# Attention's set-up over eight PSUM banks, small weights scaled earlier, and expert outputs added into the residual in DRAM

## The reference

```python
mod = silu(c) @ w_ada + b_ada                       # six vectors of 1024
h = modulate(rms_norm(x, norm1_g), sh1, sc1)
q_c, kv_c, k_r, u, b_gate, c_gate = split(h @ w_in) # 256, 128, 32, 512, 512, 512
attn = mla_mixer(...)      # 8 heads; keys 64 + 32 rotary; mask by chunks of 64
conv = b_gate * (short_conv(c_gate * u) + conv_b)
x = x + g1 * (concat(rms_norm(attn), rms_norm(conv)) @ w_out)
h2 = modulate(rms_norm(x, norm2_g), sh2, sc2)
x = x + g2 * hier_moe(h2)  # 4 groups x 8 experts, best 2 of the best group
return rms_norm(x, final_g)
```

## Time and profile before

| | us |
|---|---|
| median of 3 runs (2191.21 to 2192.27) | 2191.83 |
| profiled execution, its own time | 2191.35 |
| its span in the trace | 2189.6 |
| TensorE busy (matmul) | 1880.3, 86% |
| VectorE busy | 1234.1, 56% |
| ScalarE busy | 702.4, 32% |
| GpSimd busy | 641.9, 29% |
| data moved by DMA | 307.54 MB, 140 GB/s |

### The profile page before, as it was taken

One profiled execution on the slowest core, in us unless ns is written; L12 is line 12 of the kernel. 1 busy time (PEld: TensorE's weight loads), 2 busy tenths in 40 slices (PEclk: granted clock), 3 DMA queues, 4 the chain that ended last, 5 costly groups with the idle time before them and its releaser, 6 DMA issues. The chain is left out here.

```text
span 2189.6 us, 26611 instructions
## 1 busy us (share of the span) xinstructions
PE 1880.3 (86%) x8674; PEld 1448.1 (66%) x8674; DVE 1234.1 (56%) x1938; ACT 702.4 (32%) x1091; POOL 641.9 (29%) x662
## 2 busy tenths in 40 slices
PE   2999999937999999999997699992999999999900
PEld 2677878814656656656655488882998899998800
DVE  5667576555775775776775644435333343333359
ACT  2435343202333333333333233220223322223234
POOL 5677776601211211211211311100232333323100
PEclk9999999966999999999999699996999999999955
DMA  7555656300000000000000444424788887888478
GB/s 288 178 158 169 183 143 173 106 33 1 8 8 5 7 7 5 7 7 5 7 7 27 157 160 147 150 96 145 247 270 273 277 278 270 278 265 274 164 300 332
DMA packets 214685, 307.54 MB, mean 140 GB/s; under 512 B 22901, under 2 KB 166480, under 8 KB 212314
## 3 DMA queue, kind: packets, MB, share of 16 engines
q1 hardware_dynamic: 191002, 228.99, 32.3%
q0 software_dynamic: 18944, 69.21, 8.7%
q10 hardware_dynamic: 4672, 8.56, 1.0%
HBM read 245.91 MB, written 60.82 MB: 140 GB/s over the span
## 5 line engine op out<-in xcount | busy, mean ns | idle before, releaser
L823 PE MATMUL tbank<-KR,VV 128*128 128x512 f32 (+3 forms) x640 | 299.3, 549 | 27.2 <-DVE on L919 27.2
L1015 ACT ACTIVATE KR<-tbank 128x512 f32<-128x512 f32 (+1 forms) x320 | 170.3, 532 | 334.1 <-PE tbank L800 330.9
L903 DVE TENSOR_REDUCE cmax<-tbank 128x1 f32<-128x512 f32 (+2 forms) x340 | 205.8, 607 | 76.9 <-PE tbank L761 67.5
L1038 POOL TENSOR_SCALAR diag<-cst,nmax 128x128 fp32r<-128x128 f32 x138 | 84.1, 610 | 533.4 <-DVE nmax L906 533.4
L798 PE MATMUL tbank<-Qhi,Khi 97*128 97x512 f32 (+2 forms) x321 | 216.9, 676 | 0.0
L348 PE MATMUL pbank<-hhi,wslhi 128*128 128x512 f32 x512 | 205.5, 401 | 4.5 <-DVE wsllo L399 2.8
L1724 DVE TENSOR_SCALAR xTe<-ebank,modcol 128x256 f32<-128x256 f32 (+1 forms) x128 | 53.7, 472 | 260.4 <-PE ebank L1644 139.2
L348 PE MATMUL pbank<-hhi,wsllo 128*128 128x512 f32 x512 | 200.0, 391 | 0.0
L348 PE MATMUL pbank<-hlo,wslhi 128*128 128x512 f32 x512 | 199.6, 390 | 0.0
L1666 PE MATMUL ebank<-xTe,wg 128*128 128x192 f32 x1024 | 171.8, 326 | 3.1 <-DVE ahi L1752 1.8
L1666 PEld LDWEIGHTS ebank<-xTe,wg 128*128 128x128 f32 x1024 | 167.9, 190 | 7.8 <-DVE aT L1748 2.1
(11 more groups left out here) (261 smaller groups left out, 3517.7 us busy)
## 6 DMA issues: line engine op xcount, KB each, us to landing
wg<-in_w_exp_gate SPq DMA_DIRECT2D x32, 1024.0 KB, 5.9
wu<-in_w_exp_up SPq DMA_DIRECT2D x32, 1024.0 KB, 10.2
wd<-in_w_exp_down SPq DMA_DIRECT2D x32, 1024.0 KB, 7.7
wraw<-in_w_in SPq DMA_DIRECT2D x60, 512.0 KB, 3.8
wmod<-in_w_ada POOLq DMA_DIRECT2D x16, 1024.0 KB, 7.0
y<-y_dram SPq DMA_DIRECT2D x16, 1024.0 KB, 21.3
wada<-in_w_ada SPq DMA_DIRECT2D x2, 4096.0 KB, 22.5
xt<-in_x SPq DMA_DIRECT2D x4, 2048.0 KB, 12.4
```

What stands on the lines that cost most here:

```text
L823: ins = pe.matmul(out, VV[:, kt, 2 * b:2 * b + 2].rearrange("p c d -> p (c d)"), step_of(probs, m), start=kt == 0, stop=last)
L903: W(ve.tensor_reduce(cmax[:, i % 2, n:n + 1], plain[:, chunk % 2, 0:w], AX.X, ALU.max), plain_read)
L1015: A(act.activation(step_of(probs, m), scores[:, m % 2, j * P:512], ACT.Exp), exp_done)
```

## The change

It makes three groups of edits.

In **project**, the loads of w_uq, w_uk and w_uv come after the three broadcast rows, ahead of the loop that loads slices, and their scaling goes to VectorE at group 2, slice 14. For room, buffers are shared (`xsq` with `hf`, `uc` with `sq[:, 0]`, `t4` with `conv[:, 1]`), with three more waits, and `LATE` is 32: 32 steps of 128 columns.

In **attend**, the first head's keys go to banks 0 to 3 and its queries to banks 4 to 7, without waits between them; values follow in freed banks. Constant rows move from VectorE to ScalarE (mask rows, rotary high part) and GpSimd (zero rows, fills of VV), those of the second buffer later. `probs` has a buffer of its own.

In **route, experts and combine**, gates are split in three bfloat16 parts and carried as marks (6 x 32 columns), so that each slot has its gate. VectorE now takes both outputs out of PSUM and multiplies them by gate and g2row. GpSimd adds the rows to x2_dram with an accumulating indirect DMA; each scatter waits until the previous expert's has landed, and the b rows go for each expert apart. y_dram is gone, and combine only loads x2, normalises and stores, on SP, with four result buffers.

```diff
-LATE = 16
+LATE = 32
...
+            q = T["w_uq"].rearrange("l (k p) n -> p (l k) n", p=P)
+            sp.dma_start(wuq[:, :, 0:HEADS * QKD], q).then_inc(ld_up, 16)
...
+                    if (n, s) == (2, 14):
+                        ve.wait_ge(ld_up, 16 * 6)
+                        for k in range(KQ):
+                            V(ve.tensor_scalar(wuq[:, k], wuq[:, k], cols[:, R_Q + k:R_Q + k + 1], SM, ALU.mult, ALU.mult))
+                        V(ve.tensor_scalar(wuk[:], wuk[:], cols[:, R_KV:R_KV + 1], None, ALU.mult))
+                        V(ve.tensor_scalar(wuv[:], wuv[:], cols[:, R_KV:R_KV + 1], None, ALU.mult))
...
+            for n in range(4):
+                pe.matmul(bank[0:NOPE, n], wk[:, 0], kvn[:, n * 512:(n + 1) * 512], start=True, stop=True
+                          ).then_inc(made_done, 1)
+            for n in range(4):
+                for k in range(KQ):
+                    ins = pe.matmul(bank[:, 4 + n], wq[:, 0, k], qn[:, k, n * 512:(n + 1) * 512],
+                                    start=k == 0, stop=k == KQ - 1)
+                ins.then_inc(made_done, 1)
+            for v in range(V_EARLY):
+                pe.wait_ge(made_dve, V_EARLY_AFTER[v])
+                make_values(v, 0, bank[:, V_EARLY_BANK[v]])
...
+            rope_low(0)
             W.wait()
             for chunk in range(AHEAD):
                 maximum(chunk, chunk)
+            rope_low(1)
...
+            for n in range(4):
+                part(2 * n + 1, 0, 0)
+                if n < V_EARLY:
+                    copy_values(n, 0, bank[:, V_EARLY_BANK[n]])
+                mask_rows(0, n)
+            rope(1)
             for g in range(GROUPS_AHEAD):
                 copy_maxima(g, 0, 0)
+            for n in range(4):
+                mask_rows(1, n)
...
+            zero = cst[QKD:QKD + 1, C_ID:C_ID + 1].to_broadcast([1, S])
+            for b in range(2):
+                for k, lows in enumerate((Klo, Qlo)):
+                    po.tensor_scalar(lows[QKD:QKD + 1, b], zero, 0.0, None, ALU.mult).then_inc(rows_pool, 1)
+                    po.wait_ge(rows_pool, 2 * b + k + 1)
+                if b == 0:
+                    for k in (1, 3):
+                        po.memset(VV[:, :, k], 1.0).then_inc(filled, 1)
+                        po.wait_ge(filled, k // 2 + 1)
+                    for n in range(4):
+                        rest(n, 0, 0)
+                    po.wait_ge(qlo_done, 4)
...
+            for i, left in enumerate((gates, gleft[:, 0], gleft[:, 1])):
+                do(ve.tensor_copy(gpart[:, i], left if i else gates[:]))
+                if i < 2:
+                    do(ve.tensor_tensor(gleft[:, i], left if i else gates[:], gpart[:, i], ALU.subtract))
+                for k in range(2):
+                    do(ve.tensor_tensor(marks[:, :, k, (3 + i) * NEXP:(4 + i) * NEXP], pick[:, :, k],
+                                        across(gpart[:, i, k::2].unsqueeze(2), NT, NEXP), ALU.mult))
...
-                po.indirect_dma_start(out=y_dram, in_=y, in_offset=None,
+                po.indirect_dma_start(out=x2_dram, in_=y, in_offset=None, compute_op=ALU.add,
...
+                hold(po, st_ya[1 - b], r * (PAIRS * 16) + q * 16 + b * 16, passed_pool)
+                hold(po, st_yb[1 - b], r * (PAIRS * 16) + q * 16 + b * 16, passed_pool)
                 hold(po, ya_done, r * NEXP + q * 2 + (b + 2), passed_pool)
                 put(ya[:, b], ja[:, b:b + 1], st_ya[b])
+                hold(po, yb_done, r * NEXP + q * 2 + (b + 2), passed_pool)
+                put(yb[:, b], jb[:, b:b + 1], st_yb[b])
...
+                ve.scalar_tensor_tensor(ya[:, b], outa.rearrange("p a n -> p (a n)"),
+                                        gate_a[:, bass.ds(r * 0 + q * 2 + b, 1)], g2row[:], ALU.mult, ALU.mult
+                                        ).then_inc(ya_done, 1)
...
+            for i in range(NL):
+                sp.dma_start(x2[:, 2 * i:2 * i + 2], x2_dram[2 * i * P:(2 * i + 2) * P, :].rearrange(
+                    "(q p) d -> p q d", p=P)).then_inc(ld[i], 16)
+            for t in range(NT):
                 sp.wait_ge(normed, t + 1)
+                sp.dma_start(out_rows[t * P:(t + 1) * P, :], res[:, t % NR]).then_inc(st_out[t % NR], 16)
```

More of the change, by code:

```diff
@@ L44 @@
 ROUNDS = -(-S // CAP)
+MARKS = 6
 EPS = 1e-6
@@ L711, in _ @@
         def _(sp):
[L712 to L718, removed]
             for k in range(2):
@@ new lines, in _ @@
+            for n in range(4):
+                at = slice(n * 512, (n + 1) * 512)
+                ve.wait_ge(khi_done, n + 1)
+                W(ve.tensor_tensor(Klo[0:NOPE, 0, at], bank[0:NOPE, n], Khi[0:NOPE, 0, at].bitcast(F32),
+                                   ALU.subtract), made_dve)
+            for n in range(4):
+                at = slice(n * 512, (n + 1) * 512)
+                ve.wait_ge(made_done, 4 + n + 1)
+                ve.wait_ge(qlo_done, max(n - 1, 0))
+                W.wait()
+                W(ve.tensor_tensor(qf[0:QKD, n % 2], bank[0:QKD, 4 + n], cs[0:QKD, at], ALU.mult))
+                W(ve.tensor_tensor(turned_q[NOPE:QKD], bank[QKD:P, 4 + n], cs[QKD:P, at], ALU.mult), made_dve)
+                W.wait()
+                W(ve.tensor_tensor(qf[NOPE:QKD, n % 2], qf[NOPE:QKD, n % 2], turned_q[NOPE:QKD], ALU.add),
+                  qf_ready)
@@ L947, in _, with rope_low @@
-            for c in range(8):
-                part(c, 0, 0)
+            def rope_low(b):
+                ve.wait_ge(rope_ready, b + 1)
+                W(ve.tensor_tensor(Klo[NOPE:QKD, b], KR[NOPE:QKD], Khi[NOPE:QKD, b].bitcast(F32), ALU.subtract), rope_rest)
+            rope_low(0)
             W.wait()
@@ L1806, in _ @@
-                    ve.scalar_tensor_tensor(row[:], in_tile, 2.0, row[:], ALU.mult, ALU.add).then_inc(dve_step, 1)
-                    n += 3
-                    ve.wait_ge(dve_step, r * 10 + n)
-                    ve.scalar_tensor_tensor(dest[:], tile, 2.0 * P, row[:], ALU.mult, ALU.add
-                                            ).then_inc(table_ready, 1)
-                assert n == 10
+                            ve.tensor_copy(tab_c[half], bank[half, 5, 0:2 * NEXP].rearrange(
+                                "p (k q c) -> p k q c", k=2, c=2)[:, :, :, b]).then_inc(dve_step, 1)
@@ new lines, in _ @@
+                    ve.scalar_tensor_tensor(row[:], mark, 0.0, dump, ALU.is_equal, ALU.mult).then_inc(dve_step, 1)
+                    ve.wait_ge(dve_step, r * TABLE_STEPS + (n + 2))
+                    ve.tensor_tensor(gate[:], gate[:], tab[:, 5], ALU.add).then_inc(dve_step, 1)
+                    ve.tensor_tensor(row[:], row[:], in_tile, ALU.add).then_inc(dve_step, 1)
+                    n += 4
+                    ve.wait_ge(dve_step, r * TABLE_STEPS + n)
+                    ve.scalar_tensor_tensor(dest[:], tile, float(P), row[:], ALU.mult, ALU.add
+                                            ).then_inc(table_ready, 1)
@@ L1888, in _ @@
                 split_down(PAIRS - 1, 1, r)
-                for b in range(2):
-                    out_first(PAIRS - 1, b, r)
 def combine(nc, T, st, out):
@@ L1942, in _ @@
+            square(0)
             for t in range(NT):
                 if t + 1 < NT:
-                    first_gate(t + 1)
-                act.wait_ge(added, t + 1)
-                act.activation(junk[:], x2[:, t % NB], ACT.Square, accum_out=stat[:, t % NB, 0:1]).then_inc(squared, 1)
-                root(t)
-                if t:
-                    store(t - 1)
-            store(NT - 1)
-            for r in range(NR):
-                act.wait_ge(st_out[r], 16 * NT // NR)
+                    square(t + 1)
+                act.wait_ge(stat_step, 2 * t + 2)
+                act.activation(stat[:, t, 2:3], stat[:, t, 1:2], ACT.Sqrt).then_inc(scale, 1)
```

291 lines of the change are left out of this document (134 added, 157 removed).

## The result

The changed kernel takes 2271.17 us (median of 4 runs, 2270.13 to 2273.9) against 2191.52 for the kernel before: ratio 1.0362, interval 1.0347 to 1.0378. The forecast was 2229 in 2180 to 2310.

A forecast was written before the change was run, and what follows sets the result against it. TensorE was taken as the bound in the late projection and expert loop, but not in attention's set-up or the end. Terms 87 - 31 + 12 + 0 + 9 - 39 = +38 on 2191.35 gave 2229 us, range 2180 to 2310.

The forecast's parts named there:

- end of the projection: Projection: GpSimd's loop, cut into 32 steps, finishes at 532 us, so the stage ends 87 us later than at 445.
- attention's set-up: Barrier to first scores: keys and queries without waits between start plain scores at T+31 instead of T+65; -31 us (-40 to -18).
- combine: Last stage: 16.8 MB remain of 33.6 MB, 54 us instead of 93.3, -39 us; bounds on its length 49 and 65.
- Instructions: GpSimd's modulation loop: 240 more instructions at 0.26 us each, +62 us (50 to 80).
- Issues and pauses: GpSimd's modulation loop: 16 more load issues, store issues and pauses before the store, 1.85 us each, +30 us.
- Waits: GpSimd's modulation loop: 32 waits of 3.5 us for half-size loads against 104 us in all, +8 us (0 to +104).
- rival of long waits: GpSimd's modulation loop: half loads wait nearly as long as whole ones, +58 to +96 us, 2287 to 2325; chance 0.12.
- Stalls: GpSimd's modulation loop: 70 us lost beside VectorE's work, kept unchanged (bounds 40 and 100).
- without that cover about 4 us: Projection: its other edits cost 0 while GpSimd ends last, otherwise about 4 us.
- 3 us of extras: Attention's set-up: VectorE's 2048-column subtraction and ScalarE's eight copies ahead of the loop, of which 3 us show.
- scatter chain: Expert loop: chained scatters become the bound once a landing passes 15.3 us; +70 us, 2299; chance 0.12.
- faster rival: Projection: narrow instructions cost half and stalls shrink, so GpSimd's loop ends by 494 us; 2142 at best; chance 0.17.

The follow-up runs named there:

- before_late32: The kernel before with only LATE changed from 16 to 32 (32 steps of 128 columns in GpSimd's loop): 2314.69 us, ratio 1.0571.
- after_order: The changed kernel with GpSimd's second-buffer zero rows behind the first diagonals and ScalarE's mask rows ahead of the maxima's copies: 2268.24 us.
- after_wide: The changed kernel with 16 steps of 256 columns again, each step's columns loaded in two halves over k: 2157.55 us, ratio 0.9853.

## Why the prediction was right or wrong

The sign, the place and the mechanism were right: the loop lost its 13 us of cover, ran on alone, and all other engines stood at the barrier. The size was off by 41 us: the projection cost 46 more than forecast and the set-up gained 12 less, while table, tail and combine came out 17 better. The terms were these.

| step | forecast | measured |
|---|---|---|
| end of the projection | +87 | +133.1 |
| attention's set-up | -31 | -19.3 |
| route and table | +12 | +10.5 |
| expert loop | 0 | 0 |
| tail | +9 | +3.6 |
| combine | -39 | -48.7 |
| sum | +38 | +79.2 |

**The loop is the step that failed**: of its four terms one was right, three too small. Against the forecast's +100 the last store moved by 146:
- Instructions, forecast 62. At their minima the 256 products (0.60 us) and 224 additions (0.45 us) make 254.4 us, where 199 stood: +55. The gaps, the idle time ahead of lines 326 and 328, are 40.6 against 20.2: +20. Together 76. The rows gave 0.28 for a product and 0.18 for an addition, both borne out by the new minima, and I took the lower for both: 128 x 0.1 = 13 us.
- Issues and pauses, forecast 30: 66.1 against 36.4, +29.7. Right.
- Waits, forecast +8: 136.6 against 103.8, +33. A load waits 4.3 us on the mean (136.6 / 32) and not 3.5. The 3.5 is right for a load that runs alone: the nine behind 440 us wait 3.6 each (32.2 in sum). The 23 beside the projection wait 4.5 (104.5 in sum), and there the forecast was short. The rule of the Trainium skill ("DMA: Bandwidth & Descriptors", Anatomy of one DMA) would have had 5.3 by its 1.2 us for the half: the mean lies midway between the two. Its landing fell from 7.0 to 4.5 us, by 2.5, where the rule's slope gives 1.2 and proportion 3.5. Of the rival of long waits, +58 at the least, 25 us were real.
- Stalls, forecast unchanged at 70: 332.0 - 254.4 = 78, +8.

So 25 us lie in the waits, 14 in instructions and gaps, 8 in stalls. `before_late32` cuts the same 133 us another way: 12 come from other edits in the projection, for which the forecast had 0 as long as GpSimd ends last. They slowed the loop that ended last. They also made TensorE's part 4.1 us longer (last product at 433.71 in `before_late32`, 437.78 in the changed kernel), all of it ahead of the first product on `sq` (77.45 and 81.52), which is the forecast's "without that cover about 4 us", hidden here by the loop. The narrow instructions by themselves had made that part 8 us shorter (441.69 before), and this gain too is hidden.

**Set-up.** The first plain score was forecast at T+31 and came at T+30.3 (608.80 - 578.52). At the first score the gain is 26.1 us (81.1 to 55.0). The 3 us of extras were wrong: "GpSimd must first write two rows, so hidden" counted the first buffer's rows, and the second buffer's two rows stand in the queue between the last rest and the first diagonal. That cost 8.4 us of plain phase, as `after_order` shows. Behind the first score another 6.8 us are lost, which the forecast did not have. In its first 20 us TensorE makes 49 products at a granted clock of 0.67, where it had made 60 at 0.85; whether ScalarE's eight copies do this, and what the rest is, stays open. That the sum lies near the bound of -18, named for GpSimd's rows alone, is in part luck.

**Expert loop, scatter chain.** Both as said: 551.8 us before and after, a landing of 8.5 us, far from the 15.3 that the rival needed. **Tail**: the added landing was about zero (8.1 to 8.5 us), only the wait for the scatter before remained. **Table**: the columns bound it, +4.7 of the +5 taken. **Combine** took 44.7 us, less than the lower bound of 49 given for its length: I priced it by bytes at 360 GB/s plus 7, and it moved them at 373 with first load and last store inside the time.

The faster rival failed at both its steps: a half-wide product costs 0.60 us against 0.92 at the least, not half, and stalls did not shrink with the width.

## What to carry to other kernels

- When an edit frees SBUF by narrowing a loop on another engine, find that loop's distance to the end of its stage first. Here it was 13 us, and the half-width loop alone cost 121. The same 4 KB, with the two sums' tiles at full width, loaded in quarters gave a version 2.6% faster than before.
- Price narrower instructions kind by kind, from the minimum durations at two widths, and the wait for a load beside the traffic that it will meet: 3.6 us alone, 4.5 beside the projection.
- A hidden loop should be just hidden: GpSimd slows VectorE's instructions with two SBUF operands, and working without waits up to 421 us made TensorE's end 11 us later than pausing for loads up to 432 us did (451.7 against 440.9).

## What I had not expected

- GpSimd's density reaches TensorE through VectorE: 1.22 us for a 1024-column subtraction with GpSimd nearly idle, 1.26 with short instructions and waits between, 1.44 without waits, 1.61 with 512-column ones, and up to 21 us on TensorE's part of the projection.
- An accumulating scatter of 128 rows of 4 KB lands in 8.5 us where a plain one in the same kernel takes 6.7, and in the kernel before the plain one took 8.1: what surrounds it weighs as much as the addition.
- TensorE stood idle for 137 us at clock 0.50 ahead of attention in the changed kernel, and attention took 733.6 us. In `after_wide`, the same attention code behind a rest of 24 us, it took 733.1. The long rest did not make the stage behind it slower.
